# FFN down products as seven block products, their sums on VectorE, and the down weights loaded a turn earlier

## The reference, cut to what matters

```
y = rmsnorm(h, norm_ffn_g)                                # h: 256 x 1024
h = h + (silu(y @ w_gate) * (y @ w_up)) @ w_down           # w_gate, w_up: 1024 x 2816, w_down: 2816 x 1024
out = rmsnorm(h, norm_final_g)
```

## Time and profile before

| | us |
|---|---|
| median of 3 runs | 1141.1 (1137.57 to 1142.21) |
| profiled execution | 1141.42 |
| its span, first to last instruction | 1139.6 |
| granted TensorE clock, mean | 0.996 |
| TensorE busy | 1112.0 (98%) |
| VectorE busy | 707.6 (62%) |
| ScalarE busy | 583.6 (51%) |
| HBM traffic | 193.96 MB, mean 170 GB/s |

### The profile page before, as it was taken

One profiled execution on the slowest core, in us unless ns is written; L12 is line 12 of the kernel. 1 busy time (PEld: TensorE's weight loads), 2 busy tenths in 40 slices (PEclk: granted clock), 3 DMA queues, 4 the chain that ended last, 5 costly groups with the idle time before them and its releaser, 6 DMA issues.

```text
span 1139.6 us, 17781 instructions
## 1 busy us (share of the span) xinstructions
PE 1112.0 (98%) x7033; PEld 984.8 (86%) x7033; DVE 707.6 (62%) x997; ACT 583.6 (51%) x767; POOL 142.6 (13%) x105
## 2 busy tenths in 40 slices
PE   8899999999998999999999999999999999999997
PEld 7767888888887888888888999898899989999996
DVE  5764565565668646565656878566587566554554
ACT  5565544444579554444455546455555346443443
POOL 3543300000265240000030000000000011000001
PEclk9999999999999999999999999999999999999999
DMA  7917565555442236556545654436643545656552
GB/s 216 306 54 186 182 198 188 200 190 184 118 137 88 98 111 222 191 186 201 189 156 185 204 171 149 132 128 223 203 159 120 185 148 160 221 175 194 189 172 89
DMA packets 138782, 193.96 MB, mean 170 GB/s; under 512 B 7147, under 2 KB 112840, under 8 KB 138716
## 3 DMA queue, kind: packets, MB, share of 16 engines
q1 hardware_dynamic: 126796, 181.92, 48.4%
q10 hardware_dynamic: 11312, 11.05, 3.6%
q0 software_dynamic: 608, 0.08, 0.1%
HBM read 191.90 MB, written 6.37 MB: 174 GB/s over the span
## 4 chain that ended last, share of the span: by engine, by line
PE 83%; ACT 6%; DVE 5%; issue 2%; DMA 2%; POOL 0%; ACTq 0%; DVEq 0%; POOLq 0%
PE psum L548 20%; PE psum L549 20%; PE psum L550 20%; PE psum L709 11%; PE psum L710 5%; ACT arena L1552 3%; PE psum L637 2%; ACT whi L1566 2%; DVE wlo L2125 1%; DMA raw<-in_a_w_in 1%; PE psum L1264 1%; PE psum L668 1%; PE psum L1237 1%; DVE arena L2566 1%; DMA raw<-in_b_w_o 0%
## 5 line engine op out<-in xcount | busy, mean ns | idle before, releaser
L1566 ACT ACTIVATE whi<-raw 128x2048 fp32r<-128x2048 f32 (+2 forms) x174 | 325.9, 1875 | 255.5 <-PE psum L550 172.5
L2125 DVE TENSOR_TENSOR wlo<-raw,whi 128x2048 fp32r<-128x2048 f32 (+1 forms) x149 | 337.5, 2267 | 184.1 <-ACT whi L1566 183.2
L548 PE MATMUL psum<-xA,whi 128*128 128x256 f32 x840 | 239.8, 285 | 2.7 <-DVE wlo L2125 1.7
L549 PE MATMUL psum<-xA,whi 128*128 128x256 f32 x840 | 237.6, 283 | 0.0
L550 PE MATMUL psum<-xA,wlo 128*128 128x256 f32 x840 | 237.5, 283 | 0.0
L1535 POOL TENSOR_TENSOR wlo<-raw,whi 128x288 fp32r<-128x288 f32 (+3 forms) x56 | 112.6, 2037 | 793.8 <-ACT whi L1566 793.5
L709 PE MATMUL psum<-xA,whi 128*128 128x512 f32 x512 | 183.0, 400 | 0.0
L548 PEld LDWEIGHTS psum<-xA,whi 128*128 128x128 f32 x840 | 160.3, 191 | 6.0 <-DVE wlo L2125 3.2
L549 PEld LDWEIGHTS psum<-xA,whi 128*128 128x128 f32 x840 | 160.4, 191 | 0.7
L550 PEld LDWEIGHTS psum<-xA,wlo 128*128 128x128 f32 x840 | 160.4, 191 | 0.1
L548 PE MATMUL psum<-whi,xC 128*128 128x512 f32 (+1 forms) x384 | 149.2, 389 | 1.1 <-DVE xC L2439 1.1
(11 more groups left out here) (269 smaller groups left out, 1339.7 us busy)
## 6 DMA issues: line engine op xcount, KB each, us to landing
raw<-in_w_in SPq DMA_DIRECT2D x42, 1024.0 KB, 4.9
raw<-in_mlp_w_up SPq DMA_DIRECT2D x32, 1024.0 KB, 5.4
raw<-in_mlp_w_down SPq DMA_DIRECT2D x32, 1024.0 KB, 4.8
raw<-in_w_gate SPq DMA_DIRECT2D x11, 1024.0 KB, 5.1
raw<-in_w_up SPq DMA_DIRECT2D x11, 1024.0 KB, 5.2
raw<-in_w_down SPq DMA_DIRECT2D x11, 1024.0 KB, 4.8
raw<-in_a_w_in SPq DMA_DIRECT2D x6, 1024.0 KB, 7.1
raw<-in_a_w_o SPq DMA_DIRECT2D x4, 1024.0 KB, 4.7
```

Of the source, the lines that this page charges most:

```text
L548: nc.tensor.matmul(out, lh, rh, start=start, stop=False, skip_group_check=skip)
L549: nc.tensor.matmul(out, lh, rl, start=False, stop=False, skip_group_check=skip)
L1566: nc.scalar.activation(whi[c % N_SPLIT][:, 0:n], raw[c % N_RAW][:, 0:n], ACT.Copy).then_inc(hi_sem, 1)
L2125: V.tensor_tensor(wlo[c % N_SPLIT][:, 0:n], raw[c % N_RAW][:, 0:n], f(whi[c % N_SPLIT][:, 0:n]), ALU.subtract).then_inc(lo_sem["dve"], 1)
```

## The change

The 2 x 2 blocks of a down step's hidden tile (two k-tiles of hidden columns, two token blocks) and the 2 x 2 blocks of its weights (two k-tiles, two halves of output columns) are multiplied in Winograd's form of Strassen's scheme: seven block products, of blocks and of sums of blocks, in place of eight. The products M1 to M7 are each added over the steps in a PSUM bank of their own (1 to 7), in steps 0 to 9; step 10 is done with the plain eight block products (`four_products`), into banks 0 to 3, of which 1 to 3 already hold M4, M3 and M2. VectorE makes four sums of hidden blocks (`hidden_sums`) and four of weight blocks (`weight_sums`) in each of the steps 0 to 9. High parts are ScalarE's (`down_high`, `hidden_copy`), low parts VectorE's (`raw_low`, `sum_low`, `hidden_rest`). At the end `seven_sums` adds M1, M5, M6 and M7 into `hres` with their signs.

Gate and up products of steps 2 to 10 share bank 0; those of steps 0 and 1 stay in banks 4 to 7. TensorE's order becomes: gate 0, up 0, row scale, gate 1, up 1, six products of step 0, M7 of step 0; then turns of gate p+1, M1 M6 M7 of step p, up p+1, M5 M2 M3 M4 of step p. The down weights have two raw buffers and two split buffers of their own; the load of down 0 stands behind that of `co3` and waits until `pb1.1` is full, that of down 1 right behind up 1, later ones ahead of gate and up of the next step. In place of two buffers each for the gate and Silu there is one, in place.

```diff
...
+        down_hi = [down_split[:, 7168 * j:7168 * j + 3584] for j in range(2)]
+        down_lo = [down_split[:, 7168 * j + 3584:7168 * j + 7168] for j in range(2)]
+        wsum = area(14336, 4, 512)
+        raw_bufs = [raw[0][:, :], raw[1][:, :], down_raw[:, 0:SLOT], area(16384, SLOT)]
+        hidden = down_raw[:, SLOT:SLOT + 1024]
+        xB_flat = xB[:, :, :, :].rearrange("p s k n -> p (s k n)")
+        hidden_hi = [xB_flat[:, 2048 * j:2048 * j + 1024] for j in range(2)]
+        hidden_lo = [xB_flat[:, 2048 * j + 1024:2048 * j + 2048] for j in range(2)]
+        gate_buf, rs_row = area(18432, 512), area(18944, SEQ)
...
+        seven = {"M1": (4, 1, 0), "M2": (3, 3, 2), "M3": (2, 7, 1), "M4": (1, 2, 6),
+                 "M5": (5, 4, 3), "M6": (6, 5, 5), "M7": (7, 6, 4)}
+        SEVEN = ("M1", "M6", "M7", "M5", "M2", "M3", "M4")
...
+            def seven_products(s, p, order, loop=None, start=False, closing=None, part=None):
...
+                if part in (None, 0):
+                    pe.wait_ge(down_low_raw, count(lambda x: whole_count(s, x)))
+                    pe.wait_ge(down_low_sum, count(lambda x: sums_count(s, x)))
+                    pe.wait_ge(hidden_low, count(lambda x: whole_count(s, x)))
+                wh, wl = [w[p % 2].rearrange("p (a n) -> p a n", n=512) for w in (down_hi, down_lo)]
+                xh, xl = [v[p % 2].rearrange("p (a n) -> p a n", n=P) for v in (hidden_hi, hidden_lo)]
+                for m in order:
+                    b, x, w = seven[m]
+                    ins = three(psum[:, b, :], xh[:, x, :], xl[:, x, :], wh[:, w, :], wl[:, w, :], start, True, True)
+                    if closing and b >= 4:
+                        close_bank(ins, f"{closing}.{m}")
+                if part in (None, 1):
+                    ins.then_inc(seven_done, 1)
+            def four_products(s, n):
+                p = down_steps[s] - 1
+                pe.wait_ge(down_low_raw, whole_count(s, p))
+                pe.wait_ge(hidden_low, whole_count(s, p))
...
+            wide_step("g1", 5, low[index["ffn.g1"]], None)
+            wide_step("u1", 7, low[index["ffn.u1"]], None)
+            open_seven("F")
+            pe.wait_ge(gate_scaled, 2)
+            seven_products(2, 0, ("M2", "M3", "M4", "M1", "M5", "M6"), None, True, None, 0)
+            pe.wait_ge(hidden_step, hidden_count(2, 1, 1))
+            seven_products(2, 0, ("M7",), None, True, None, 1)
...
+            def ffn_turn(p, loop=None, closing=None, cut_at=3):
...
+                wide_step(f"g{p + 1}", 0, count(lambda x: low[index[f"ffn.g{x + 1}"]]), (hidden_step, count(free_up)))
+                seven_products(2, p, SEVEN[:cut_at], loop, False, closing, 0)
+                wide_step(f"u{p + 1}", 0, count(lambda x: low[index[f"ffn.u{x + 1}"]]),
+                          (gate_scaled, count(lambda x: x + 2)))
+                seven_products(2, p, SEVEN[cut_at:], loop, False, closing, 1)
+            ffn_turn(1)
...
+                    static(index["ffn.d0"])
+                    for x in range(3):
+                        for kind in ("gu", "gud", "gu")[x]:
+                            static(index[f"ffn.{kind}{x}"])
                     with sp.Fori(0, 4) as r:
                         for q in range(2):
...
+                            for kind, view, first in (("d", wd, 2), ("g", wg, 3), ("u", wu, 3)):
+                                js = [first + 2 * y + q for y in range(4)]
+                                ring([index[f"ffn.{kind}{j}"] for j in js], view, js, kind == "d", r)
...
+                        static(index["ffn.d0"])
...
+            def down_high(s, p, loop=None):
...
+                act.wait_ge(raw_sem[raw_of[c]], count(lambda x: landed[down_chunk(s, x)]))
+                if p >= 2:
+                    act.wait_ge(seven_done, count(lambda x: sums_count(s, x - 2)))
+                nc.scalar.activation(down_hi[p % 2][:, 0:1536], raw_bufs[raw_of[c]][:, 512:SLOT],
+                                     ACT.Copy).then_inc(down_high_raw, 1)
+                act.wait_ge(down_sum, count(lambda x: 3 * sums_count(s, x)))
+                nc.scalar.activation(down_hi[p % 2][:, 1536:3584], wsum.rearrange("p a n -> p (a n)"),
+                                     ACT.Copy).then_inc(down_high_sum, 1)
+            def hidden_copy(s, p, loop=None):
...
+                last = p == down_steps[s] - 1
+                act.wait_ge(hidden_step, count(lambda x: hidden_count(s, x, 1 if last else 4)))
+                if p >= 2:
+                    act.wait_ge(seven_done, count(lambda x: sums_count(s, x - 2)))
+                v = slice(0, 512) if last else slice(P, 1024)
+                nc.scalar.activation(hidden_hi[p % 2][:, v], hidden[:, v], ACT.Copy).then_inc(hidden_high, 1)
+            def first_copy(n):
+                act.wait_ge(*full[f"{n}.M1"])
+                nc.scalar.activation(wsum[:, 0, :], psum[:, 4, :], ACT.Copy).then_inc(read[f"{n}.M1"][0], 1)
...
+            def ffn_step(p, loop=None):
+                hidden_copy(2, p, loop)
+                down_high(2, p + 1, ahead_of(loop))
+                gate_silu(p + 1, ahead_of(loop))
+                for w in "gu":
...
+            def hidden_sums(s, p, loop=None):
...
+                x = hidden.rearrange("p (a n) -> p a n", n=P)
+                step(2, V.tensor_tensor(x[:, 6, :], x[:, 0, :], x[:, 1, :], ALU.subtract))
+                step(3, V.tensor_tensor(x[:, 4:6, :], x[:, 0::6, :], x[:, 2:3, :].to_broadcast([P, 2, P]), ALU.subtract))
+                V.tensor_tensor(x[:, 7, :], x[:, 3, :], x[:, 5, :], ALU.add).then_inc(hidden_step, 1)
+            def weight_sums(s, p, loop=None):
...
+                c = down_chunk(s, p)
+                at = [landed[down_chunk(s, x)] for x in (loop[0] if loop else (p,))]
+                dve.wait_ge(raw_sem[raw_of[c]], along(at, loop[1]) if loop else at[0])
+                b = raw_bufs[raw_of[c]].rearrange("p (a n) -> p a n", n=512)
+                step(1, V.tensor_tensor(wsum[:, 0:2, :], b[:, 0:1, :].to_broadcast([P, 2, 512]), b[:, 1:3, :], ALU.add))
+                step(2, V.tensor_tensor(wsum[:, 2, :], b[:, 1, :], wsum[:, 1, :], ALU.add))
+                V.tensor_tensor(wsum[:, 3, :], b[:, 3, :], wsum[:, 2, :], ALU.add).then_inc(down_sum, 1)
+            def sum_low(s, p, loop=None):
...
+                dve.wait_ge(down_high_sum, along(at, loop[1]) if loop else at[0])
+                V.tensor_tensor(down_lo[p % 2][:, 1536:3584], wsum.rearrange("p a n -> p (a n)"),
+                                f(down_hi[p % 2][:, 1536:3584]), ALU.subtract).then_inc(down_low_sum, 1)
+            def raw_low(s, p, loop=None):
...
+                dve.wait_ge(down_high_raw, along(at, loop[1]) if loop else at[0])
+                a, n = (0, SLOT) if p == down_steps[s] - 1 else (512, 1536)
+                V.tensor_tensor(down_lo[p % 2][:, 0:n], raw_bufs[N_RAW + p % 2][:, a:a + n], f(down_hi[p % 2][:, 0:n]),
+                                ALU.subtract).then_inc(down_low_raw, 1)
+            def hidden_rest(s, p, loop=None):
...
+                dve.wait_ge(hidden_high, along(at, loop[1]) if loop else at[0])
+                v = slice(0, 512) if p == down_steps[s] - 1 else slice(P, 1024)
+                V.tensor_tensor(hidden_lo[p % 2][:, v], hidden[:, v], f(hidden_hi[p % 2][:, v]),
+                                ALU.subtract).then_inc(hidden_low, 1)
+            def seven_sums(n):
+                def scaled(b, half, src, scale, then=None):
+                    h = hres[:, b, 512 * half:512 * half + 512]
+                    run(V.scalar_tensor_tensor(h, src, scale[:, b:b + 1], h, ALU.mult, ALU.add), then)
+                run(V.tensor_scalar(minus_scale, late_scale, -1.0, None, ALU.mult))
+                dve.wait_ge(*read[f"{n}.M1"])
+                dve.wait_ge(*full[f"{n}.M6"])
+                run(V.tensor_tensor(wsum[:, 1, :], psum[:, 6, :], wsum[:, 0, :], ALU.add), read[f"{n}.M6"])
+                scaled(1, 1, wsum[:, 0, :], late_scale)
+                dve.wait_ge(*full[f"{n}.M7"])
+                run(V.scalar_tensor_tensor(wsum[:, 2, :], psum[:, 7, :], -1.0, wsum[:, 1, :], ALU.mult, ALU.add), read[f"{n}.M7"])
+                scaled(1, 0, wsum[:, 1, :], minus_scale)
+                dve.wait_ge(*full[f"{n}.M5"])
+                scaled(1, 0, psum[:, 5, :], late_scale)
+                scaled(0, 0, psum[:, 5, :], late_scale, read[f"{n}.M5"])
+                scaled(0, 0, wsum[:, 2, :], minus_scale)
+                scaled(0, 1, wsum[:, 2, :], late_scale)
...
+            def gate_scale(p, loop=None):
+                dve.wait_ge(gu_full, count(lambda x: 2 * x + 1, p, loop))
+                V.tensor_tensor(gate_buf.rearrange("p (a b) -> p a b", b=SEQ),
+                                psum[:, (4, 5)[p] if p < 2 else 0, :].rearrange("p (a b) -> p a b", b=SEQ),
                                 rs_row.unsqueeze(1).to_broadcast([P, 2, SEQ]), ALU.mult).then_inc(gate_scaled, 1)
...
```

(59 more changed lines are left out.)

299 lines of the change are left out of this document (180 added, 119 removed).

## The result

The changed kernel takes 1150.91 us (median of 4 runs, 1149.66 to 1151.4) against 1140.17 us before (4 runs, 1137.57 to 1142.21): a ratio of 1.0099, 95% interval 1.008 to 1.0118, so 10.7 us slower. The prediction was 1147.0, +5.9 us, with 1145 to 1149 as the forecast's own range: the result lies above that. The direction was right and the first turn and the end cost what was worked out; a term of 4 to 5 us was missing, from a place that the prediction never looked at.

The account below looks back on a forecast made before the run. TensorE, busy 98% of the span, was taken as the bound; 2.9 (its path) + 2.5 (the end) + 0.4 (clock) = +5.8 us gave 1147.0 us, forecast's own range 1145 to 1149, overall range 1139 to 1151.

Parts of the forecast that it names:

- the first turn: FFN start: TensorE waits for VectorE twice, 5.85 us for gate scale 1 and 3.6 us for product 1.
- the end: Kernel's tail: VectorE's combining and residual adds move the mean from 0.5 before TensorE's end to 2.05 behind, +2.5 us.
- Products removed: FFN down steps: ten of eleven do seven block products for eight, 6.8 us less of TensorE, later turns 16.29 us.
- The 0.2 for starting again: FFN's first turn: a weight load before the first product after a wait may add 0.2 us, counted once.
- Clock: FFN's first turn: the 5.85 us wait lowers TensorE's clock; cost between 0 and 1.7 us, taken as 0.4.
- the path's sum: TensorE's path through the FFN: +5.85 + 3.6 + 0.2 - 6.8 = +2.9 us.
- some 2 us of room in steady turns: Steady FFN turns: VectorE is busy 14.7 of 16.29 us, with some 2 us of room; TensorE stays the bound.
- Rival 2: FFN turns: VectorE becomes the bound of every turn; with 3 us more a turn, 1158 us; chance 0.08.
- Sum for the FFN, +5.8 us: All terms together: 2.9 for TensorE's path, 2.5 for the end and 0.4 for the clock, +5.8 us.
- the first turn was not covered: Denies the rival that VectorE's idle time covers the FFN's first turn: 1137.1 us, chance 0.12.
- the clock did not fall a second time: Denies the rival of a clock fall behind the second wait or in TensorE's first loops: 1148.3 us, chance 0.10.
- Rival 4: FFN loop: change not fully as described; waits keep seven products from running together, some 0.2 us a turn, 1149; chance 0.06.

Follow-up runs that it names:

- aligned: The changed kernel with a 32-byte pad ahead of xC, which also moves down_raw, arena and down_split: 1146.29 us, ratio 1.0055.
- eight: The aligned kernel with M4's three products done twice in steps 1 to 9, so eight groups again: 1151.58 us, ratio 1.0085.
- early: The aligned kernel with weight sums, high and low parts of down step 0 made ahead of the late norm: 1141.04 us, ratio 1.0012.
- start: The early kernel with the first turn's work on VectorE and ScalarE ordered by due time: 1138.82 us, ratio 0.9982.

## Why the prediction was partly right, and short by half

- **Products removed, 6.8 us.** Right: turns of 16.32 in aligned for 16.29, and 0.68 for a group (eight).
- **The first turn, waits of 5.85 + 0.2 and 3.6 us.** Right in place, releaser and size: 6.15 us, and 0.92 behind slowed products. The 0.2 for starting again came from no row; the first product starts 0.47 us behind the end of gate scale 1, M7 0.06 behind the end of product 1. That these two are the loss is shown by early and start.
- **Clock, 0 to 1.7, taken as 0.4.** Right in kind: it fell in the first wait, and the second wait hid the loss. In aligned, TensorE goes from the first product of gate 0 to its last in 190.59 us (942.40 to 1132.99), before in 187.70 (943.79 to 1131.49). That is +2.9, the path's sum without a term for the clock, so little or nothing is left for the 0.4.
- **VectorE has some 2 us of room in steady turns.** Right: 1.7. Rival 2 decides there, as said, and did not happen.
- **The end, +2.5 us.** Right: 2.4 by the trace. Taking it away gave 3.2 by the medians, with an uncertainty of some 2 us, and 1.7 by the traces.
- **Sum for the FFN, +5.8 us.** In aligned it is 5.3 from 940 us to the end (2.9 of TensorE's path, 2.4 of tail), and 6.2 by the medians.
- **What failed** is the sum itself, "2.9 + 2.5 + 0.4 = +5.8", which has no term outside the FFN. The prediction's account of the costs went through products, sums, loads and the end, and passed over the one hunk that reaches all stages: the new places of `xC`, `down_raw` and `arena`. It should have said that the MLPs take their stationary tile from `xC` in 32 steps and bounded that cost; it took it as nothing without a word. Measured, it is 4.0 us in the MLPs, and 16.39 for 16.32 us in the FFN's turns, 0.6 in all. 5.3 + 4.0 + 0.6 = 9.9; the medians differ by 10.7, with an interval of 9.1 to 13.5.
- None of the rivals held: the first turn was not covered, VectorE does not bound, the clock did not fall a second time. Rival 4's 0.2 us a turn for waits is not there (0.03).

## What to carry to other kernels

A change that moves a buffer is a change to every stage that reads it: keep tiles that TensorE reads on multiples of 128 bytes (32, 64 and 96 off all cost time here), and when a stage whose work is unchanged drifts, look at addresses before anything else. Where an engine has little room in a steady loop, its first turn, with nothing prepared, is a stall by itself; write the first turns out by due time and prepare what has already landed in earlier idle time. A saving of products is worth its full time only if the sums that replace them stand in the idle time of the engine that makes them, in the first and the last turn too.

## What the hardware showed that I had not expected

- With the stationary tile `xC` 32, 64 or 96 bytes past a multiple of 128, 24 products of 512 columns took 5.59 to 5.62 us, for 5.47 on a multiple. How much a whole MLP drifts (about 1.5, 0.8 and 1.9 us in 16 steps, 0.07 or less at multiples of 128) does not follow from that alone: the up products between them, which do not read `xC`, got shorter by 0.03 to 0.09 us a step. Why is open.
- The streamed operand's place seems to count too: with `xB` (stationary) unmoved and `down_split` 96 bytes off, the 21 products of a turn took 4.89 us for 4.81 in aligned; `down_raw` and `arena` moved with it, so this is less isolated.
- The first loads vary: single runs of one layout stand up to 5 us apart by 100 us into the run. The difference to before also moves by up to 1.9 us between 290 and 430 us, in kernels of either layout. Only differences between two points of one run told the 2 us effects apart.
